# End of the second feed-forward product: where p is loaded and turned, and which buffers hold W2's quarters of the last product

## The reference, cut to what matters

```python
x = layer_norm(DEEPNORM_ALPHA * x + mix, ln1_g[i], ln1_b[i])
hid = jnp.square(jax.nn.relu(jnp.einsum('bsd,df->bsf', x, ffn_w1[i])))
x = layer_norm(DEEPNORM_ALPHA * x + jnp.einsum('bsf,fd->bsd', hid, ffn_w2[i]), ln2_g[i], ln2_b[i])
gate = jax.nn.sigmoid(jnp.einsum('bsd,de->bse', x, ple_gate_w[i]))
x = x + gate * jnp.einsum('bsk,kd->bsd', p[i], ple_w[i])
```

## Time and profile before

| | |
|---|---|
| time, median of 3 runs | 2124.36 us (2123.57 to 2124.47) |
| the profiled execution | 2122.74 us, of which 2121.0 us are the span |
| PE busy | 2102.9 us, 99% of the span |
| DVE, ACT, POOL busy | 60%, 37%, 35% |
| granted TensorE clock, mean | 1.000 |

### The profile page before, as it was taken

The page is one execution under the profiler, slowest core; times in us unless marked ns, Lnnn a source line. Parts: engine busy times, 40 slices in busy tenths (PEclk is TensorE's granted clock), DMA queues, the critical chain, the costliest instruction groups (busy, mean ns, idle before and its releaser), DMA issues.

```text
span 2121.0 us, 27192 instructions
## 1 busy us (share of the span) xinstructions
PE 2102.9 (99%) x10565; PEld 1786.2 (84%) x10565; DVE 1270.7 (60%) x1747; ACT 792.8 (37%) x1197; POOL 733.5 (35%) x493
## 2 busy tenths in 40 slices
PE   9999999999999999999999999999999999999999
PEld 9887788888888888899888888788888888888899
DVE  5744776565667666565543352676556667666564
ACT  3112464544544334521211101454454543344521
POOL 5112157777512000212432222258777512000220
PEclk9999999999999999999999999999999999999999
DMA  5121124444599743301121111124444599643311
GB/s 184 39 62 46 35 80 149 141 148 163 180 361 380 248 155 129 129 26 46 41 80 40 57 43 48 32 80 161 155 141 148 203 381 378 228 131 130 129 38 73
DMA packets 185948, 287.31 MB, mean 135 GB/s; under 512 B 12800, under 2 KB 82524, under 8 KB 185820
## 3 DMA queue, kind: packets, MB, share of 16 engines
q1 hardware_dynamic: 185120, 285.26, 39.4%
q10 hardware_dynamic: 700, 0.31, 0.1%
HBM read 221.56 MB, written 63.96 MB: 135 GB/s over the span
## 4 chain that ended last, share of the span: by engine, by line
PE 91%; DVE 3%; DMA 2%; issue 1%; POOL 1%; ACT 1%; SPq 0%; DVEq 0%; POOLq 0%; ACTq 0%
PE bank_a L1785 16%; PE bank_a L1787 16%; PE bank_a L1786 16%; PE bank_b L1785 14%; PE bank_b L1787 14%; PE bank_b L1786 14%; PE bank_a L1824 1%; DMA w_raw<-in_ffn_w_dram 1%; DMA p_n<-in_p_dram 1%; PE bank_b L1824 1%; DVE xt_lo L1339 0%; DVE xt_hi L1334 0%; POOL op_lo L983 0%; PE bank_a L1994 0%; DMA h_spill<-h_tile 0%
## 5 line engine op out<-in xcount | busy, mean ns | idle before, releaser
L968 POOL TENSOR_TENSOR w_lo<-raw,w_hi 128x512 fp32r<-128x512 f32 x160 | 226.3, 1446 | 986.0 <-ACT w_hi L1072 985.9
L1785 PE MATMUL bank_a<-xt_hi,w_hi 128*128 128x512 f32 x640 | 251.4, 393 | 2.7 <-DVE xt_lo L1339 2.7
L1787 PE MATMUL bank_a<-xt_hi,w_lo 128*128 128x512 f32 x640 | 249.2, 389 | 0.0
L1786 PE MATMUL bank_a<-xt_lo,w_hi 128*128 128x512 f32 x640 | 249.1, 389 | 0.0
L1526 DVE TENSOR_TENSOR hop_lo<-h_raw,hop_hi 128x1024 fp32r<-128x1024 f32 x112 | 141.6, 1265 | 141.8 <-ACT hop_hi L1165 141.6
L1165 ACT CAST hop_hi<-h_raw 128x1024 fp32r<-128x1024 f32 x112 | 117.7, 1051 | 237.4 <-PE bank_a L1787 140.6
L1785 PE MATMUL bank_a<-wop_hi,hop_hi 128*128 128x512 f32 x512 | 199.3, 389 | 0.7 <-DVE resid L1551 0.7
L1786 PE MATMUL bank_a<-wop_lo,hop_hi 128*128 128x512 f32 x512 | 199.2, 389 | 0.0
L1787 PE MATMUL bank_a<-wop_hi,hop_lo 128*128 128x512 f32 x512 | 199.2, 389 | 0.0
L1072 ACT CAST w_hi<-raw 128x512 fp32r<-128x512 f32 x160 | 88.2, 620 | 266.1 <-PE bank_a L1787 154.7
L1785 PE MATMUL bank_b<-w_hi,xt_hi 128*128 128x256 f32 x640 | 182.4, 285 | 2.3 <-DVE xt_lo L1339 1.7
(11 more groups left out here) (190 smaller groups left out, 4961.9 us busy)
## 6 DMA issues: line engine op xcount, KB each, us to landing
w_raw<-in_ffn_w_dram SPq DMA_DIRECT2D x144, 512.0 KB, 7.6
h_raw<-h_spill SPq DMA_DIRECT2D x112, 512.0 KB, 6.5
h_spill<-h_tile SPq DMA_DIRECT2D x170, 256.0 KB, 2.2
w_raw<-in_ffn_w_dram SPq DMA_DIRECT2D x112, 256.0 KB, 3.5
raw<-in_od_w_in_dram SPq DMA_DIRECT2D x48, 256.0 KB, 2.8
raw<-in_ple_gate_w_dram SPq DMA_DIRECT2D x32, 256.0 KB, 4.8
h_spill<-h_tile2t SPq DMA_DIRECT2D x28, 256.0 KB, 2.0
raw<-in_ev_w_in_dram SPq DMA_DIRECT2D x24, 256.0 KB, 3.1
```

What stands on the lines that cost most here:

```text
L968: pool.tensor_tensor(w_lo[slab % 2][:, s], raw[:, n % NRAW, :], w_hi[slab % 2][:, s].bitcast(F32), ALU.subtract).then_inc(lo_split, 1)
L1785: pe.matmul(dst, s_hi, m_hi, start=first, stop=False, skip_group_check=on_top)
L1786: pe.matmul(dst, s_hi, m_lo, start=False, stop=False, skip_group_check=on_top)
L1787: return pe.matmul(dst, s_lo, m_hi, start=False, stop=last, skip_group_check=on_top)
```

## The change

It has four parts. The W2 quarters of items 48 to 55 are kept in two buffers in turn (128, 132) instead of four (128, 168, 172, 132, 128, 132, 168, 172). The load of `p_n` moves from `second` to `slab`, ahead of the first gate slab, and waits for `dve[47]`. The eight transposes of p, ACT's copies and DVE's splits of them become a stage of their own, after item 53 and before `second`. ACT's first cast for the second slab waits for `dve[55]` and no longer for `sum[55]`, since the slab's low parts lie over buffers 128 and 132.

```diff
--- before.py
+++ after.py
@@ -189,7 +189,7 @@
     def w_chunk(self, load):
         if load < self.first_load[LAST_FORM]:
             return (184, 188, 32, 36, 168, 172, 176, 180)[load % 8]
-        return (128, 168, 172, 132, 128, 132, 168, 172)[load - self.first_load[LAST_FORM]]
+        return (128, 132)[(load - self.first_load[LAST_FORM]) % 2]
 
     def w_landed(self, load):
         return load % 8, 16 * (self.layer * self.loads // 8 + load // 8 + 1)
@@ -434,9 +434,9 @@
             if i == LAST_FORM + 3:
                 add("slab", layer=layer, load_next=True, split_next=True)
             if i == LAST_FORM + 5:
+                add("turn_p", half=0, layer=layer)
                 add("second", layer=layer)
-        st.inner = [add("turn_p", half=0, layer=layer, nested=True, early=True)]
-        squares_of(hi).inner = st.inner
+        squares_of(hi)
         add("stats", half=1, ln=ln)
         add("norm", half=1, ln=ln)
 
@@ -843,13 +843,13 @@
                 if st.kind == "slab":
 
                     sp.wait_ge(ahead_dve, ahead[st.layer].dve[LAST_FORM - 1])
+                    sp.dma_start(p_n[:, :, :], p[st.layer, 0].rearrange("(t q) k -> q t k", q=P)).then_inc(p_in, 16)
                 if st.load_next and st.cur + 1 < n_slabs:
                     load_slab(*slabs[st.cur + 1])
                 if st.kind == "second":
 
                     load_slab(slabs[st.cur + 2][0], st.piece + 5)
                     sp.wait_ge(ahead_dve, ahead[st.layer].dve[-1])
-                    sp.dma_start(p_n[:, :, :], p[st.layer, 0].rearrange("(t q) k -> q t k", q=P)).then_inc(p_in, 16)
                     load_gb(ln2_g[st.layer], ln2_b[st.layer], D)
                 if st.kind == "ffn":
                     for k in range(2):
@@ -1137,7 +1137,7 @@
                 if st.kind == "split":
                     split_high(st.cur + 2, st.piece + 4, 4, slab_end[st.cur])
                 if st.kind == "second":
-                    act.wait_ge(ahead_dve, ahead[st.layer].sum[-1])
+                    act.wait_ge(ahead_dve, ahead[st.layer].dve[-1])
                     split_high(st.cur + 2, st.piece + 5, 4)
                     split_high(st.cur + 2, st.piece + 9, 1, at=4)
                 if st.kind == "consts":
@@ -1263,7 +1263,7 @@
                         act.wait_ge(dve_const, PAD)
                         act.activation(table[:, st.sums:st.sums + 1], inv_cnt[:, 0:1], ACT.Sqrt)
                     for k, t in enumerate(st.tiles):
-                        if k == (1 if st.kind == "square" else len(st.tiles) - 1):
+                        if k == len(st.tiles) - 1:
                             for turn in st.inner:
                                 values(turn)
                         act.wait_ge(mean_ready, st.sq + k + 1)
@@ -1534,9 +1534,6 @@
                     if form == "m1":
                         dve.wait_ge(acc_ready, st.accd)
                     for k in range(HT):
-                        if k == HT - 2:
-                            for turn in st.inner:
-                                put(turn, (0, 1))
                         if FORMS[form][0] == "A":
                             dve.wait_ge(a_full, head.ga + k + 1)
                             src = bank_a[(head.ga + k) % RING][:, :]
@@ -1873,9 +1870,6 @@
                     items = (i - 1, i) if i == len(ITEMS) - 1 else (i,)
                     pe.wait_ge(ahead_dve, a.dve[i])
                     for k in range(HT):
-                        if k == 2:
-                            for turn in st.inner:
-                                turn_groups(turn, range(2))
                         if ITEMS[i][1] == 0:
                             dst = free_bank(ring, st, k)[:, :]
                         else:
```

## The result

The changed kernel takes 2143.03 us (median of 6, 2141.01 to 2143.60) against 2124.41 us before, a ratio of 1.0088 with a 95% interval of 1.0078 to 1.0099. The change makes the kernel 18.6 us slower. In the profiled execution the span is 2141.6 us and the mean granted clock 0.996.

The account below looks back on a forecast made before the run. PE, busy 99% of the span, was taken as the bound. Per layer, stall 8.7, clock 2.0 and second wait 2.5 us, twice, less 3.7 for p, gave +22.7 us on the median of 2124.36: 2147.1, range 2134 to 2156.

Parts of the forecast that it names:

- p's wait goes: PE's waits for `p_n`, one in each layer, vanish because p is loaded earlier; gain 3.7 us in all.
- A closed chain: From item 50 on, W2 loads and DVE wait for each other; a round costs 3.58 us plus landing L, 7.8 us.
- The flush of `m7` stands behind the chain: DVE flushes `m7` only after `wop_lo` of item 51, so PE stands still before item 48, 8.7 us per layer.
- The second wait: PE waits at item 55, after the transposes of p, about 2.5 us per layer.
- The clock: After the stall before item 48 PE's first matmuls run slower, 2.0 us per layer, bounds 0 and 2.7.
- Rival 1: PE keeps its full clock through the stall: 4.0 us less, 2143 us; chance 0.2.
- Item 55 behind the gate slab on ACT: Gate pieces queue behind p, ACT casts them before preparing item 55, so PE waits about 2.5 us per layer.
- Second slab, squares and `gb_rows` cost nothing: The second slab's later casts, ACT's squares behind them and the later `gb_rows` load cost PE no time.
- Rivals 2 to 4: 2: flush in time, 2120.7 us, chance 0.03; 3: own line; 4: loads land in 6 us each, 2161, chance 0.05.
- Rival 3: The flush doesn't hold PE, only the wait at item 55 is new: about +3.7 us, 2128 us; chance 0.06.

Follow-up runs that it names:

- The cheaper move: Kernel before, with p's load issued ahead of the fifth piece of the second gate slab; 2118.42 us, ratio 0.9979.
- the kernel that kept PE busy: Changed kernel with 28 extra matmuls before item 48, their result unread; 2140.11 us, ratio 1.0075 to the kernel before.
- Two experiments on the mixed buffers: Mixed buffers with four gate pieces ahead of p, fifth behind: 2119.98 us; mixed buffers with stage `slab` behind item 55's preparation: 2118.88 us.
- mixed buffers: Changed kernel with four W2 buffers for items 48 to 51 as before, two for the rest, p waiting for item 50; 2123.42 us, ratio 1.0000.
- flush first: Changed kernel with item 51's preparation and item 52's `wsum` moved behind item 47 and the flush of `m7`; 2123.91 us, ratio 1.0004.
- the two buffers alone: Kernel before with only the two W2 buffers and ACT's later wait, p left where it was; 2150.06 us, ratio 1.0126.

## Why the prediction was right

2147 us were forecast with a range of 2134 to 2156, and 2143.03 measured. Step by step:

- **p's wait goes, 3.7 us.** Right: no wait for `p_n` is left. The cheaper move shows that the gain was to be had without the rest.
- **A closed chain with 3.58 + L us a round.** Right in mechanism. The size of L was off: the quarters of items 49 to 52 landed 3.9, 3.6, 3.8 and 3.9 us after issue, and I had taken 4.2. `wop_lo` of item 51 ended at 845.78, forecast 847.6.
- **The flush of `m7` stands behind the chain.** Right, and shown: with the flush moved ahead of the chain's last round the stall is gone, though the loads are as slow. The term was 8.7 us per layer and measured 7.0. Of the terms this one was furthest off, 3.4 us in both layers. The second wait was taken 1.2 us too high and the clock 1.9 too low, so the terms measured 20.0 against 22.7 forecast. Between these 20.0 and the 18.6 of the medians lie the untraced 0.6 us and the scatter of the two profiled executions.
- **The clock.** 2.0 us per layer taken, 2.2 and 2.0 measured. The granted clock of 0.50 in the rows and the kernel that kept PE busy both say so. The rule of the Trainium skill ("TensorE: Matmul & The Clock Gate", "Why this matters for your kernels"), that a gap of idle PE brings the half rate back, agrees with these rows. Rival 1 fell, although its 2143 us is the time that was measured. That is chance: the stall came out 3.4 us smaller than forecast, while rival 1 leaves out 4.0 us of clock that were there. Nor did speak for rival 1, as the slices of 53 us don't show a stretch of 4 us; a closer view of the kernel before does read 1.00 in the first 5 us, where the transposes were slow, and what slowed them stays open.
- **Item 55 behind the gate slab on ACT.** Right nearly to the us: the quarter of item 55 was forecast for 870.5 and issued at 870.59, the fifth cast was to end at 884.2 and did at 884.31, `wop_lo` was forecast for 887.7 and ended at 888.22. This closeness is partly luck. I had shifted this part by 8.7 us of stall without the slow matmuls, and the shorter stall and the slow matmuls together made 9.2. ACT's first cast began 0.9 us later than forecast (879.01 against 878.1), and from there to the end of the fifth took 5.3 us and not 6.1. The terms were 2.5 per layer, measured 2.3 and 1.5. Not forecast was that the clock falls a second time, behind this shorter wait, for 1.7 us in layer 0. Two experiments on the mixed buffers show the cause from both sides, the loads and ACT's order.
- **Second slab, squares and `gb_rows` cost nothing.** Right: PE has no wait for them.
- **Rivals 2 to 4.** None held; the quarters landed neither within 2 us nor in 6. Rival 3's place was real in another form: with the chain made harmless, the change wins 3.7 us and loses 3.5 or 3.1 (mixed buffers, flush first), which is no change.

## What to carry to other kernels

Fewer buffers lengthened no operation here, they closed a loop: a load waits for the consumer, and the consumer's engine waits for the load, so compare one round with the pace of the engine that bounds. Then look at what stands behind the waiting instruction in that engine's list, since here the chain itself was harmless and only the flush behind it cost 14 us of waiting, and 4.2 more in slow matmuls. And before a load is moved far ahead, see which single wait in its queue holds it; here, putting p one load ahead, before the piece that waits, won 4.2 us with the buffers left alone.

## What the runs showed of the hardware that was not expected

- The granted clock fell to its lower level behind a gap of PE of 2.3 us with eight transposes ahead of it (layer 0, clock 0.54 from 888.3 to 892.0), but not behind one of 1.5 us in layer 1. In the kernel before it didn't fall behind waits for p of 1.2 and 2.5 us. In the kernel that kept PE busy it fell behind a wait of 2.3 us in layer 1 only after PE had worked again for 0.8 us at 1.00, and was 0.54 from 2004.1 to 2007.8. What makes the difference was not tried.
- The same stall didn't always cost the same: behind waits of 6.7 to 7.4 us for the flush, 10 or 11 matmuls were slow in the changed kernel (2.0 and 2.2 us) and 14 with the two buffers alone (2.9 us in each layer). This too was not tried apart.
- `hop_lo` on DVE took 1.79 us at 885.29, where it took 1.22 elsewhere. POOL was making the slab's low parts until 886.0; that this is the cause was not tried apart.
